# A fused attention and gating layer on 8 cores: PSUM banks picked by a modelled earliest-free time instead of in turn

## The reference

```python
h = rmsnorm(x, norm_g)
proj = h @ w_in + b_in                                  # 1024 -> 2816 columns
q, k, v, z_a, u_s, v_s, z_s = split(proj)               # 512,128,128,512,512,512,512
attn = banded_sink_attention(q, k, v, sinks) * silu(z_a)   # 8 query heads, 2 kv heads, window 128
u_s, v_s = gelu(u_s), gelu(v_s)
sgu = u_s * (tril(W_s) @ layernorm(v_s) + b_s) * silu(z_s) # per chunk of 128, 8 heads
x = x + concat(attn, sgu) @ w_out + b_out
return rmsnorm(x, final_norm_g)
```

## Time and profile before

| | |
|---|---|
| time, median of 3 runs | 667.02 us |
| time of the profiled execution | 666.81 us |
| its span, slowest core (core 3) | 665.3 us |
| spans of the 8 cores | 653.3 to 665.3 us |
| PE busy | 552.1 us, 83% |
| ACT busy | 371.7 us, 56% |
| DVE busy | 295.4 us, 44% |
| POOL busy | 230.2 us, 35% |

### The profile page before, as it was taken

One profiled execution on the slowest core, in us unless ns is written; L12 is line 12 of the kernel. 1 busy time (PEld: TensorE's weight loads), 2 busy tenths in 40 slices (PEclk: granted clock), 3 DMA queues, 4 the chain that ended last, 5 costly groups with the idle time before them and its releaser, 6 DMA issues.

```text
span 665.3 us, 9869 instructions; the slowest of 8 cores (653.3 to 665.3 us)
## 1 busy us (share of the span) xinstructions
PE 552.1 (83%) x3042; PEld 243.7 (37%) x3042; DVE 295.4 (44%) x556; ACT 371.7 (56%) x729; POOL 230.2 (35%) x224
## 2 busy tenths in 40 slices
PE   0299468899798988899798988899798988899682
PEld 0143233444334443444334443444334443444130
DVE  0410363445544463435544454435544454435444
ACT  0423565548754695547754695547753595544643
POOL 0464581346016141345016141245116151254010
PEclk9999798999898998999898998989898998989798
DMA  7997800230014100330014100330013100110002
GB/s 225 270 326 265 128 0 18 110 127 1 1 64 148 45 1 13 114 127 0 1 64 137 53 1 9 119 127 1 1 64 130 63 0 1 65 65 0 1 32 95
DMA packets 15750, 50.11 MB, mean 75 GB/s; under 512 B 2513, under 2 KB 2769, under 8 KB 15698
## 3 DMA queue, kind: packets, MB, share of 16 engines
q1 hardware_dynamic: 14546, 47.38, 20.8%
q0 software_dynamic: 1152, 2.10, 2.2%
HBM read 34.79 MB, written 16.78 MB: 78 GB/s over the span
## 4 chain that ended last, share of the span: by engine, by line
PE 49%; ACT 18%; issue 10%; POOL 7%; DVE 6%; DMA 6%; SPq 2%; POOLq 0%; ACTq 0%; DVEq 0%
PE pb L361 26%; PE pb L540 10%; PE pb L403 7%; ACT PT L448 5%; DMA y_t<-w_in 5%; ACT LR L482 4%; DVE y_t L548 3%; POOL LR L487 3%; ACT LR L486 2%; ACT junk L554 2%; PE pb L441 2%; POOL st_rs L306 2%; DMA gf_sb<-gf_bc 1%; PE pb L405 1%; ACT junk L297 1%
## 5 line engine op out<-in xcount | busy, mean ns | idle before, releaser
L361 PE MATMUL pb<-xT,w_in_bf 128*128 128x512 bf16 x1088 | 260.2, 396 | 16.8 <-ACT LR L486 14.7
L361 PEld LDWEIGHTS pb<-xT,w_in_bf 128*128 128x128 bf16 x1088 | 106.8, 101 | 157.8 <-issue 48.3
L540 PE MATMUL pb<-w_out_bf,mixT 128*128 128x512 bf16 x512 | 129.2, 411 | 7.1 <-DVE mixT L491 4.6
L487 POOL TENSOR_TENSOR LR<-LR,zaT 128x512 f32<-128x512 f32 x32 | 36.9, 1153 | 269.0 <-ACT LR L486 269.0
L554 ACT ACTIVATE junk<-y_t 128x1024 bf16<-128x1024 f32 x32 | 33.8, 1057 | 119.6 <-DVE y_t L548 119.6
L329 POOL TENSOR_TENSOR x_t<-x_t,bout_sb 128x1024 f32<-128x1024 f32 x32 | 82.1, 2597 | 0.0
L540 PEld LDWEIGHTS pb<-w_out_bf,mixT 128*128 128x128 bf16 x512 | 50.9, 104 | 81.8 <-issue 36.8
L450 DVE TENSOR_TENSOR PT<-PT,mask_sb 128x512 bf16<-128x512 bf16 x126 | 52.4, 425 | 38.2 <-ACT PT L448 32.9
L448 ACT ACTIVATE PT<-pb 128x512 bf16<-128x512 f32 x126 | 63.9, 612 | 0.0
L403 PE MATMUL pb<-w_in_bf,xT 128*128 128x512 bf16 x256 | 60.7, 380 | 0.0
L491 DVE TENSOR_TENSOR mixT<-pb,LR 128x512 bf16<-128x512 f32 x32 | 22.1, 692 | 85.5 <-POOL LR L487 81.3
(11 more groups left out here) (59 smaller groups left out, 517.9 us busy)
## 6 DMA issues: line engine op xcount, KB each, us to landing
x_t<-x SPq DMA_DIRECT2D x32, 512.0 KB, 4.0
out<-y_t SPq DMA_DIRECT2D x32, 512.0 KB, 2.7
x_t<-w_in SPq DMA_DIRECT2D x10, 512.0 KB, 8.6
y_t<-w_in SPq DMA_DIRECT2D x6, 512.0 KB, 8.3
x_t<-w_in SPq DMA_DIRECT2D x6, 384.0 KB, 8.7
w_out_bf<-w_out POOLq DMA_DIRECT2D x8, 256.0 KB, 10.1
y_t<-w_in SPq DMA_DIRECT2D x2, 384.0 KB, 6.0
x_t<-sgu_wT SPq DMA_DIRECT2D x1, 512.0 KB, 11.0
```

The lines of the kernel that those rows point to most:

```text
L361: ins = e.matmul(pbank[b][:], lhsT=w_in[:, k, col:col + 128], rhs=xT[:, k, :], start=(k == 0), stop=(k == 7))
L487: S.op("pool", lambda e: e.tensor_tensor(out=LR[:, lb, :].rearrange("p (c q) -> p c q", c=4), in0=LR[:, lb, :].rearrange("p (c q) -> p c q ...
L540: ins = e.matmul(pbank[b][:], lhsT=mixT[:, ec, tt * 128:(tt + 1) * 128], rhs=w_out[:, ec, hf * 512:(hf + 1) * 512], start=(ec == 0), stop= ...
```

## The change

The counter goes. `newbank()` keeps a model in numbers written by hand: `pe_now`, the time at which TensorE would be done with what was issued so far, and `free_at` for each bank. It picks the bank with the smallest `free_at`, lets TensorE's modelled work start when the bank is free, advances `pe_now` by `pe_dur` and sets the bank free `hold` later. The calls pass their own `pe_dur` and `hold`, and `exclude` keeps the banks of one unit apart. The model knows TensorE's durations and one fixed hold per kind of use; it does not know what the reading engine has queued ahead of the read. No instruction is added or taken away and none changes its place on any engine: what changes is which of the six banks each group of matmuls writes, and so which earlier read it waits for. Lines shift by 6 or 7 in the changed kernel (L361 becomes L368, L382 becomes L389, L386 becomes L393, L540 becomes L547).

```diff
--- before.py
+++ after.py
@@ -193,12 +193,18 @@
         d_y = [sem(f"d_y{i}") for i in range(2)]
 
         S = Sched(esems)
-        bank_ctr = [0]
-
-        def newbank():
-            b = bank_ctr[0] % NB
-            bank_ctr[0] += 1
+        pe_now = [0.0]
+        free_at = [0.0] * NB
+
+        def newbank(pe_dur=1.85, hold=0.9, exclude=()):
+            b = min((i for i in range(NB) if i not in exclude), key=lambda i: free_at[i])
+            start = max(pe_now[0], free_at[b])
+            pe_now[0] = start + pe_dur
+            free_at[b] = pe_now[0] + hold
             return b
+
+        def pe_advance(dur):
+            pe_now[0] += dur
 
         consts = [
             ("c_gcol", gcol[:], gcol_d), ("c_biasfm", bias_fm[:], biasfm_d), ("c_bv", bv_bc[:], bv_d),
@@ -269,7 +275,7 @@
         S.op("act", lambda e: e.activation(out=esink_col[:], in_=esink_col[:], func=AF.Exp), reads=["c_sink"], writes=["esink_col"])
         S.op("dve", lambda e: e.tensor_copy(out=bvs_row[:], in_=bvs_f[:]), reads=["c_bvs"], writes=["bvs_row"])
 
-        cb = newbank()
+        cb = newbank(0.5, 3.0)
 
         def cmat_mm(e):
             ins = None
@@ -341,6 +347,7 @@
                         for c in range(8):
                             ins = e.transpose(pt[:, c, :], xn[:, tt, c * 128:(c + 1) * 128], ident[:])
                         return ins
+                    pe_advance(0.6)
                     S.op("pe", tr, reads=[("xn", tt), "c_ident"], writes=[("psT", tt % 2)])
                     S.op("dve", lambda e: e.tensor_copy(out=xT[:, :, tt * 128:(tt + 1) * 128], in_=pt[:]),
                          reads=[("psT", tt % 2)], writes=[("xT", tt)])
@@ -374,7 +381,7 @@
             def mkv(tt):
                 def unit():
                     n = 4 * st + tt
-                    b = newbank()
+                    b = newbank(0.6, 0.7)
 
                     def mmv(e):
                         ins = None
@@ -395,7 +402,7 @@
 
             def mkvs(tt):
                 def unit():
-                    b = newbank()
+                    b = newbank(2.1, 1.0)
                     vb = tt % 2
 
                     def mmvs(e):
@@ -432,7 +439,7 @@
                 sbk = {}
                 for g in range(2):
                     for kb in kbs:
-                        b = newbank()
+                        b = newbank(0.25, 1.0 + 0.5 * (2 * g + kb), exclude=set(sbk.values()))
                         sbk[(g, kb)] = b
                         kn = n - 1 + kb
                         kslot = kn % 8
@@ -457,8 +464,8 @@
                 zb = st % 2
                 pp = n % 2
                 kbs = [1] if n == 0 else [0, 1]
-                bn_ = newbank()
-                bd_ = newbank()
+                bn_ = newbank(0.6, 5.5)
+                bd_ = newbank(0.6, 2.0, exclude={bn_})
 
                 def mmpv(e):
                     for g in range(2):
@@ -497,7 +504,7 @@
         def D_units(st):
             def mk(jj):
                 def unit():
-                    b = newbank()
+                    b = newbank(0.5, 1.0)
 
                     def mmg(e):
                         ins = None
@@ -531,7 +538,7 @@
                     mkeys = [("mixA", tt)] + [("mixS", jj) for jj in range(4)]
                     banks = []
                     for hf in range(2):
-                        b = newbank()
+                        b = newbank(1.75, 2.0 + 1.75 * (1 - hf), exclude=set(banks))
                         banks.append(b)
 
                         def mmo(e, hf=hf, b=b):
```

## The result

The changed kernel takes 695.27 us (median of 10 runs) against 667.15 us: a ratio of 1.042, 95% interval 1.0406 to 1.0433. The forecast was 700, range 690 to 707. (One of the ten runs before, 690.9 us, and two of the ten after, 705.63 and 737.18 us, the latter two with a lower granted clock on one die, are left out of the ratio.) The profiled execution took 694.74 us.

A forecast was written before the change was run, and what follows sets the result against it. PE, busy 83% of the span, was taken to bound the kernel. New v wait 31.5 us plus second projection tile 3.2 less last stage 1.1 gave 33.6 us on 666.81: 700 us, range 690 to 707.

The forecast's parts named there:

- The wait that comes: Fourth v unit waits for the first's late-queued v_r read; PE idles 6.4 us, output 4.5 us later, 31.5 us in all.
- The wait that goes: Third v unit writes DEN's bank, not PV's, so its 1.82 us wait for the mixT write goes.
- The second new wait: Second projection tile waits 0.46 us for the read of the first one's bank, paid in full: 3.2 us.
- The others: First block's PV and remaining groups return to banks freed in time: nothing, upper bound 3.5 us.
- The clock at the new stop: At the output behind the v units, 1.67 us of slow clock per stage stays; bounds 11.7 us less, 7 more.
- The clock at the first tile: First projection tile keeps 1.53 us of slow clock per stage; some of 10.7 us may be given back.
- The last stage: Second block's PV no longer waits for mixT, third block's DEN waits for an exp: 1.1 us gained, bounds 0 and 1.7.
- Rival 1: At the v units, v_r reads served promptly, stop and its slow clock vanish: 24.5 us saved, 644 us; chance 5%.
- The small idles: By the skill's rule the new 0.46 us wait brings a slow tile, some 10.5 us more; the prediction did not adopt it.

The follow-up runs named there:

- e2: Kernel before, banks in turn, with only the fourth v unit taking the first v unit's bank (the two swapped from there on): 695.19 us, ratio 1.0416.
- e1: Changed kernel with one number altered, the v units' hold 5.5 instead of 0.7: 665.13 us, ratio 0.9965 to the kernel before.
- e4: Changed kernel, same banks, with the four v_r reads ahead of the third block's scaling tail on VectorE: 672.00 us, ratio 1.0064 to the kernel before.
- e3: Kernel before with only the second projection tile taking the first one's bank (the two swapped from there on): 666.76 us, ratio 0.9981.
- e5: Changed kernel with 26 overwritten matmuls of 512 columns ahead of the third v unit's own, in its bank: 691.05 us, ratio 1.0331 to the kernel before.
- e6: Kernel before, banks in turn, with the four v units writing quarters of one bank, read by one VectorE operation: 648.89 us, ratio 0.9709.
- e10: e6 with eight overwritten matmuls of 512 columns ahead of the first projection tile, in its bank: 644.47 us, ratio 0.9653 to the kernel before.

## Why the prediction was right

- **The wait that comes** was right in place, length and count: 6.4 us forecast, 6.45 to 6.5 seven times; 4.5 us per stage forecast, 4.55 read. Within it two small errors cancel: the fourth v unit was taken at full clock (0.55 us) and took 1.01, so that the output starts 4.7 us later and not 4.5, and the output took 5.15 us and not 5.30. e2 shows it alone, e1 its absence, e4 that the read's place in VectorE's queue makes it.
- **The wait that goes**: right, the third unit follows the first two without a gap.
- **The second new wait**: 0.46 forecast, 0.46 read in the stage shown. That it is paid in full holds in the changed kernel's timeline and in the stage lengths of e3 and e1 (0.4 to 0.55 us per stage at the same clock); the time of e3 as a whole shows nothing of it.
- **The others** cost nothing, as taken: PV of the first block follows without a wait.
- **The clock at the new stop**: the 1.67 kept from before was right (5.15 for 5.30, and e5 puts it back to 3.62), with 0.4 more on the fourth v unit, which the 4.5 us include.
- **The clock at the first tile** is the term that was mis-sized. I kept 7 x 1.53 and named giving it back as the lower end; it was given back in six of seven stages, 9 us. The fall comes a few us earlier within the stage and stretches matmuls that had to wait afterwards anyway. These 9.2 us less, 2.3 more in the last stage and 1.3 more ahead of the first make 695 of 700. That the misses partly cancel is luck; the forecast's main term stands without it.
- **The last stage**: -1.1 forecast, +1.2 read. I followed the wait for the exp, 1.25 us after the exps begin, but not that PE had nothing to do ahead of it: 4.13 us idle, and then two outputs at the slow clock (5.64 and 5.30 us for 3.61).
- **Rival 1** was rightly held unlikely, but its price was wrong. Without the stop e1 takes 665, not 644, for the fourth v unit waits for mixT and the output for a residual read next; with the v_r reads served earlier, which is what the rival supposed, e4 takes 672. The 3.5 us per stage are only to be had when v takes fewer banks (e6: 2.8).
- **The small idles** that the Trainium skill warns of (TensorE: Matmul & The Clock Gate, section "A second HAM failure mode: psum-queue depth-cycling") brought no slow tile of their own here, as the prediction held against that rule: behind the waits of 0.39 and 0.89 us in the changed kernel the work runs at full clock (1.89 us for the tile, 3.63 for the output). No run shows whether they have a part in the falls elsewhere in the stage.

## What to carry to other kernels

A model that hands out buffers must know when the reader is served, not how long its read takes: an in-order engine may have a chain queued ahead of it. Here one hold of 0.7 us stood for a bank that was busy for 7.3 (its matmuls ended at about 444.1, its read at 451.4), and cost 28 us, while the other choices of the model gained nothing that e1 shows beside the clock. Before tuning who gets which bank, look at who holds one longest and for how little; four units that used a quarter of a bank each, packed into one, gave 2.9%. And price a stop with its clock: a kernel may pay the half clock in a wait, where it is free, or in a matmul tile, where it is not, so a few us per stage can come or go with an edit that only shifts the stage. Compare stages in the same clock before a small gain is put down to the edit.

## What the runs showed that was not expected

The same program settled into different patterns of the clock. Before, each stage of core 3 took 75.1 us and paid the slow clock at both places (1.53 and 1.67 us); core 5, after the same 2.05 us wait, had a full-clock tile in three of its seven stages and ended 12 us earlier. With stages of 78.5 us the first tile ran at full clock on all eight cores from the second stage on, and the cores came within 4 us of each other. Why a core settles into one pattern or the other is not shown. Useless matmuls can pay: 8 per stage, 1.90 us of PE in a wait of 2.1, made the kernel 0.6% faster (e6 to e10), while 26 per stage in the larger stop saved about 1.5 us on the output (3.62 for 5.15) and gave much of it back on the next tile.
